# A two-block float32 layer on one core: the first output projection's banks, weight buffers and row order rearranged

## The reference

```python
x = _layer_norm(x, ln_emb_g, ln_emb_b)
proj = x @ w_in                                   # q_a k_a v_a f_a | q_r f_r i_r g_r
o_a = _rms_norm_heads(_fox_attention(q, k, v, logf_a))       # 8 heads of 64
o_r = _rms_norm_heads(_hgrn2_chunked(...)) * silu(g_r)       # 4 heads of 128
mix = concatenate([o_a, o_r]) @ w_o                          # 1024 x 1024
x = _layer_norm(ALPHA * x + mix, ln_mix_g, ln_mix_b)         # ALPHA = 2 ** 0.25
h = causal_depthwise_conv(x @ w_up)                          # 1024 x 5632, width 3
a, u = split(h)
x = _layer_norm(ALPHA * x + (gelu(a) * u) @ w_down, ln_ffn_g, ln_ffn_b)
x = second_block(x, ...)
```

## Time and profile before

| | us |
|---|---|
| median of three runs | 1674.93 (1673.72 to 1675.19) |
| the profiled execution, its own time | 1673.51 |
| its span, first to last instruction | 1671.7 |
| PE busy (matmuls) | 1591.8 |
| DVE busy | 1012.8 |
| ACT busy | 698.3 |
| POOL busy | 417.9 |

### The profile page before, as it was taken

The page is one execution under the profiler, slowest core; times in us unless marked ns, Lnnn a source line. Parts: engine busy times, 40 slices in busy tenths (PEclk is TensorE's granted clock), DMA queues, the critical chain, the costliest instruction groups (busy, mean ns, idle before and its releaser), DMA issues. The chain is left out here.

```text
span 1671.7 us, 21242 instructions
## 1 busy us (share of the span) xinstructions
PE 1591.8 (95%) x8600; PEld 1335.6 (80%) x8600; DVE 1012.8 (61%) x1443; ACT 698.3 (42%) x1012; POOL 417.9 (25%) x350
## 2 busy tenths in 40 slices
PE   5999988989999999999999999999799999999997
PEld 5778876767878888788888778887688899999886
DVE  6665546557977577433776544336864688886334
ACT  5644345543533243322542334444443654544222
POOL 0024302330621111100053012223432455551002
PEclk8999999999999899999999999999999999999999
DMA  7242212352244345222346423323444022234221
GB/s 291 101 143 85 76 63 76 113 203 101 83 170 160 143 151 200 103 101 83 117 152 252 126 76 100 108 81 107 176 148 182 26 102 102 102 114 146 94 76 51
DMA packets 47068, 203.93 MB, mean 122 GB/s; under 512 B 14352, under 2 KB 14736, under 8 KB 28346
## 3 DMA queue, kind: packets, MB, share of 16 engines
q1 hardware_dynamic: 37346, 171.84, 28.8%
q0 software_dynamic: 9088, 30.38, 5.3%
q10 hardware_dynamic: 536, 0.35, 0.1%
HBM read 181.56 MB, written 21.00 MB: 121 GB/s over the span
## 5 line engine op out<-in xcount | busy, mean ns | idle before, releaser
L557 PE MATMUL ps<-xh,whi 128*128 128x512 f32 (+1 forms) x1120 | 401.0, 358 | 5.7 <-DVE wlo L1801 5.3
L559 PE MATMUL ps<-xh,wlo 128*128 128x512 f32 (+1 forms) x1120 | 395.0, 353 | 0.0
L558 PE MATMUL ps<-xl,whi 128*128 128x512 f32 (+1 forms) x1120 | 393.6, 351 | 0.0
L1801 DVE TENSOR_TENSOR wlo<-raw,whi 128x2048 fp32r<-128x2048 f32 x93 | 233.3, 2509 | 137.7 <-ACT whi L1189 137.6
L1189 ACT ACTIVATE whi<-raw 128x2048 fp32r<-128x2048 f32 (+1 forms) x191 | 237.9, 1250 | 151.3 <-PE ps L559 104.3
L557 PEld LDWEIGHTS ps<-xh,whi 128*128 128x128 f32 x1120 | 212.1, 189 | 46.2 <-issue 11.6
L559 PEld LDWEIGHTS ps<-xh,wlo 128*128 128x128 f32 x1120 | 211.5, 189 | 31.4
L558 PEld LDWEIGHTS ps<-xl,whi 128*128 128x128 f32 x1120 | 212.8, 190 | 28.9
L2211 DVE SCALAR_TENSOR_TENSOR xr<-ps,pc,xr 128x511 f32<-128x511 f32 x88 | 65.2, 747 | 45.9 <-ACT xr L1189 44.3
L2619 POOL TENSOR_TENSOR act<-xr 128x512 f32<-128x512 f32 x22 | 39.2, 1782 | 204.6 <-DVE xr L2211 203.8
L2517 DVE TENSOR_TENSOR wlo<-raw,whi 128x512 fp32r<-128x512 f32 x98 | 77.7, 824 | 0.5 <-ACT whi L1189 0.5
(11 more groups left out here) (449 smaller groups left out, 3585.8 us busy)
## 6 DMA issues: line engine op xcount, KB each, us to landing
raw<-in_w_in SPq DMA_DIRECT2D x35, 1024.0 KB, 5.1
raw<-in_ffn_w SPq DMA_DIRECT2D x33, 1024.0 KB, 4.8
raw<-in_ada SPq DMA_DIRECT2D x24, 1024.0 KB, 4.8
raw<-in_w_up SPq DMA_DIRECT2D x22, 1024.0 KB, 4.8
raw<-in_w_down SPq DMA_DIRECT2D x11, 1024.0 KB, 4.7
xd<-X POOLq DMA_DIRECT2D x8, 512.0 KB, 7.7
td<-vr POOLq DMA_DIRECT2D x16, 256.0 KB, 3.6
raw<-td SPq DMA_DIRECT2D x4, 1024.0 KB, 5.4
```

The lines of the kernel that those rows point to most:

```text
L557: pe.e.matmul(o, lh, rh, start=start, stop=False)
L558: pe.e.matmul(o, lh, rl, start=False, stop=False)
L559: return pe.e.matmul(o, ll, rh, start=False, stop=stop)
L1801: up(ve.e.tensor_tensor(lo, raw[conv_at[j] % 3][:, :], hi.bitcast(F32), ALU.subtract), "wlo")
```

## The change

Six things.

1. **Banks.** The projection's column half 0 takes its four banks, and mix tile 7 its one, from the pool "attention" (as all of the attention's tiles); column half 1 goes on with "all". The bank that a take hands out, and so the signal that PE waits for, changes for all of the projection and for the transposes behind it.
2. **Mix tile 7** is turned after the first two row tiles of quarter `J_WO` and not after all four. On ACT the rounding of mix tiles 5 and 6 and the copy of `J_WO + 1` come before the last two evictions of the spectrum.
3. **Mix tiles 0 to 3** have their turn in steps 11 to 14 instead of 9 to 12, on PE, DVE and ACT.
4. **Buffers.** `J_WO + 3` and `J_UP + 2` get the place over `qa` and `ka` that `J_UP` had, and `J_UP` uses a shared pair.
5. **Row order on DVE.** Gain and bias, first half, second half, statistics and scale go by row tiles, interleaved, and not each step over all four tiles. `WO_RES` numbers the signals of the new order.
6. **Down operands.** The first three of `ah` and `al` are made ahead of the last pair's evictions.

The diff, cut to what the prediction speaks of:

```diff
-J_AHEAD = (J_UP, J_K2, J_UP2)
+J_AHEAD = (J_WO + 3, J_UP + 2, J_K2, J_UP2)
...
-                    if 9 <= i <= 12:
-                        pe.wait_ge(sig["rec"], i - 8)
-                        mix_turn(i - 9, tiles_of(orr, i - 9))
+                    if 11 <= i <= 14:
+                        pe.wait_ge(sig["rec"], i - 10)
+                        mix_turn(i - 11, tiles_of(orr, i - 11))
...
             rows_by(J_WO, wo_tiles(0), lambda kg, t: pe.wait_ge(sig["sp_lo"], split_no("mix", 4 * kg + 3)),
-                    between=lambda: last_mixed(3))
+                    after=lambda n: None if n else last_mixed(3), pool="attention")
             rows_last(J_WO + 2, wo_tiles(1), after_wo)
...
-                    if j == J_UP:
-                        ac.wait_ge(sig["pe"], at["w", J_WO])
+                    if j in (J_WO + 3, J_UP + 2):
+                        ac.wait_ge(sig["pe"], at["w", J_WO + 3 if j > J_WO + 3 else J_WO])
...
             head_squares(7, oa, 3)
-            spectrum(14)
+            mix_high(5)
             head_roots(ms_f[:, 24:32], 64, 8)
-            mix_high(5)
-            spectrum(15)
             mix_high(6)
             high(J_WO + 1)
+            spectrum(14)
+            spectrum(15)
             mix_high(7)
...
+                    if (j2, part) == (10, 1):
+
+                        ac.wait_ge(sig["ch_lo"], 20)
+                        ac.wait_ge(sig["act"], 3)
+                        for k in range(3):
+                            act(dn1[k][0][:, :], act1[:, k, :], ACT.Copy, "sp_hi")
...
+            gained(0)
+            gained(1)
+            wo_first(0)
+            wo_first(1)
+            gained(2)
+            low_parts(J_UP)
+            wo_stats(0)
+            gained(3)
+            inverse(1, 0)
+            wo_first(2)
+            wo_stats(1)
+            wo_first(3)
+            inverse(1, 1)
+            wo_stats(2)
+            inverse(1, 2)
             channels(4)
             channels(5)
             wo_stats(3)
...
+                    if (j2, part) == (10, 1):
+                        for k in range(3):
+                            low_part(dn1[k][1][:, :], act1[:, k, :], dn1[k][0][:, :], "down0", k)
```

More of the change, by code:

```diff
@@ L150 @@
 LAST = (0, 0), (1, 0), (0, 1), (1, 1), (2, 0), (2, 1), (3, 0), (3, 1)
+WO_RES = {k: n + 1 for n, k in enumerate(((0, 0), (1, 0), (0, 1), (2, 0), (1, 1), (3, 0), (2, 1), (3, 1)))}
 def weight_plan(ins, td):
@@ L474, in build @@
         raw_sem = [sig["raw0"], sig["raw1"], sig["raw2"]]
-        ahead = {J_UP: (flat(qa_r), flat(ka_r)), J_K2: (flat(qn_r), flat(qt_r)),
+        ahead = {J_WO + 3: (flat(qa_r), flat(ka_r)), J_UP + 2: (flat(qa_r), flat(ka_r)), J_K2: (flat(qn_r), flat(qt_r)),
                  J_UP2: (flat(cl), flat(act2_r[:, 0:4, :]))}
@@ L593, in tile, with rows_by @@
                 done(o, key)
-            def rows_by(j0, tiles, ready, after=None, between=None):
-                bs = [take(key, name, value) for key, name, value, *_ in tiles]
+            def rows_by(j0, tiles, ready, after=None, between=None, pool=None):
+                bs = [take(key, name, value, pool) for key, name, value, *_ in tiles]
                 for kg in range(2):
@@ L792, in gather, with mix_turn @@
                 done(m, ("ao", i))
-            def mix_turn(n, x):
-                b = take(("mix", n), "mx_m", n + 1)
+            def mix_turn(n, x, pool=None):
+                b = take(("mix", n), "mx_m", n + 1, pool)
                 turn(("mix", n), b, x)
@@ L847, in last_mixed @@
                 pe.wait_ge(sig["hn_x"], 5 + k)
-                mix_turn(4 + k, tiles_of(oa, k))
+                mix_turn(4 + k, tiles_of(oa, k), "attention")
             for k in (1, 2):
@@ L863, in wo_tiles @@
             def wo_tiles(cg):
-                return [(("wo", t, cg), "res", 4 * cg + t + 1, mix_hi, mix_lo, t) for t in range(4)]
+                return [(("wo", t, cg), "res", WO_RES[t, cg], mix_hi, mix_lo, t) for t in range(4)]
             def mix_rows(t):
@@ L1480, in scalar_program, with pieces @@
                         channels(u)
-            def pieces(inst, src, dn, ready, first):
+            def pieces(inst, src, dn, ready, first, begun=0):
                 def one(k):
@@ L1495, in one @@
                     act(dn[k % 4][0][:, :], src[:, k, :], ACT.Copy, "sp_hi")
-                for k in range(4):
+                for k in range(begun, 4):
                     one(k)
@@ L1502, in pieces @@
                         one(k + 4)
-            pieces(0, act1, dn1, "act", lambda k: k + 1)
+            pieces(0, act1, dn1, "act", lambda k: k + 1, begun=3)
             def rows_1(t):
@@ L2134, in beside_fox @@
                     head_scale(orr, i - 6, 1, ms_r[:, 4 * (i - 6):4 * (i - 6) + 4], 1)
-                if 9 <= i <= 12:
-                    mix(i - 9)
+                if 11 <= i <= 14:
+                    mix(i - 11)
                 if i in (13, 20, 28):
@@ L2174, in residual, with gained @@
                 up(ve.e.scalar_tensor_tensor(out=x, in0=x, scalar=ALPHA, in1=b[:, :], op0=ALU.mult, op1=ALU.add), "res")
-            low_parts(J_WO + 2)
+            low_parts(J_WO + 3)
             ve.wait_ge(sig["rows"], 64)
-            for t in range(4):
+            def gained(t):
                 ve.wait_ge(sig[("x0", "x1d", "x2", "x3")[t]], 32)
@@ L2243, in pieces @@
                         one(k + 4)
-            pieces(0, act1, dn1)
+            pieces(0, act1, dn1, begun=3)
             def down_stats(t):
```

14 lines of the change are left out of this document (4 added, 10 removed).

## The result

| | before | after |
|---|---|---|
| median of the runs beside each other | 1674.5 (1673.7 to 1675.2, 4 runs) | 1658.0 (1653.3 to 1659.1, 4 runs) |
| ratio, 95% interval | | 0.9895 (0.9884 to 0.9907) |
| the profiled execution, its own time | 1673.51 | 1653.27 |
| its span | 1671.7 | 1651.4 |

The time, 1658.0, lies inside the range (1651 to 1663) and 2 us above the forecast of 1656; the gain is 16.5 us.

The account below looks back on a forecast made before the run. PE, busy 95% of the span, was taken as the bound, so time is won only at its stops or low clock. 4.1 + 9.5 + 4.7 = 18.3 off the median gives 1656.6, forecast as 1656, range 1651 to 1663.

Parts of the forecast that it names:

- A: Attention: turning mix tiles 0 to 3 two steps later gains 4.1 us, bounds 2.5 and 6.5.
- B: First projection up to the up product: its changes gain 9.5 us, bounds 7.5 and 10.4.
- C: Down product's start: three operands made earlier remove PE's stop and low clock, 4.7 us, bounds 3.1 and 4.9.
- low part to 289.7: Attention, step 11: DVE's low part, taken as 2.93 us, ends at 289.7; PE then waits 0.6 for a bank.
- DVE as the bound: Attention, steps 11 to 15: DVE's work comes together, waits equal those removed; gain there 0.5, time 1660; chance 13%.
- the four-step sums: Attention, steps 9 to 12 and 13 to 16: each four steps would take 13 or 14 us.
- The rule on the port: Projection, mix tile 7: the page's exclusive lock would make PE wait 1.4 us, 1657.5 instead of 1656; forecast kept 1656.
- I take 379.7: Projection: the last broadcast row lands at 379.7, within 378 to 381.7, a loss of 0.4 us.
- Late rows: Projection: broadcast rows land at 381.7, DVE's list 2.4 late, PE waits over 3 us; 1658.5; chance 15%.
- That `J_WO + 3` has a place of its own changes nothing here: First projection: this weight buffer's separate place gains nothing, since both copies wait for the same point.
- given back in the up product: Up product: DVE and POOL, not PE, are the bound; the projection's gain falls to about 2, 1664; chance 4%.
- denser matmuls: Whole kernel: the denser PE is granted less clock; 0.015 less gives 1679; chance 1%.

Follow-up runs that it names:

- hold_pool: The kernel after, with POOL's spectrum additions held back until DVE's low part in step 11 and, at the attention's end, until mix tile 4 is read: 1652.65, ratio 0.9873.
- buffers_undone: The kernel after with the weight buffers of before (`J_UP` over `qa` and `ka`, `J_WO + 3` and `J_UP + 2` in shared pairs): 1660.32, ratio 0.9915.
- mix_only: The kernel before with only mix tiles 0 to 3 turned in steps 11 to 14: 1672.6, ratio 0.9994.
- down_only: The kernel before with only the first three down operands made ahead of the last evictions: 1670.81, ratio 0.998.
- projection_only: The kernel after without the later mix tiles and the earlier down operands, leaving the first projection's banks, buffers and row order: 1662.41, ratio 0.9936.
- after_again: The kernel after, unchanged, run again as the measure for its group: 1657.27, ratio 0.9901.

## Why the prediction was right, point by point

**The total** was right, and it was so in part because errors cancelled. By term: A 4.1, measured 1.2 to 1.4. B 9.5, measured 8.0 in the trace up to the up product (the shift goes from +1.2 to -6.8), and 1.5 more behind it, since PE no longer stops for `xl` and keeps its clock. C 4.7, measured 4.8 at its place and 3.1 in the median. And 2.6 us in the traces, 3.6 in the median, that no term had, from the second block's attention. That the 2.7 us missing from A and this gain elsewhere nearly cancel is luck.

**Part A, the failed step.** It was "low part to 289.7", which took DVE's 2.93 from the earlier trace rows and set it in a new place. The 2.93 from 292.74 was the last 0.8 of an addition of POOL's, from 292.25 to 293.53, and 2.1 of its own. Two steps on, PE being earlier, POOL has its additions at hand just behind the products, and both fall on the same low part: 0.6 until they begin, 2.5 for both, 2.2 for itself. From there the reasoning held. The rival *DVE as the bound* came near in its outcome (waits of 2.50 and 0.45 where there were 3.21, 0.32 and 0.45, and 1.2 us of gain, not 0.5), but not in its cause, DVE's own work coming together: `hold_pool` takes no work from DVE, and the 2.50 goes. Of the signs named, the four-step sums were to be 13 or 14 us: they are 14.9 and 13.2. The trace of before had the rows that would have told it: that addition, and DVE's low part of a mix tile, 0.69 alone, that took 2.00 while POOL's products of the earlier trace rows ran to 286.7.

```profile
285.25 2.00 DVE L1806 TENSOR_TENSOR gcr<-mx,qrr 128x512 fp32r<-128x512 f32 x1 [0.70 <-ACT qrr L1189]
...
292.25 1.28 POOL L2619 TENSOR_TENSOR spo<-spe,spo 128x512 f32<-128x512 f32 x1
```

**The rule on the port** was weighed against a row, and the row was misread. In all of them DVE ends when POOL's instruction has ended and DVE's own time, less some 0.14, has passed: 285.25 + 2.00 is POOL's end at 286.71 and 0.54 (0.69 alone), 360.00 + 1.52 of the earlier trace rows is POOL's end at 360.98 and 0.54, 292.74 + 2.93 is 293.53 and 2.14 (2.29 alone), 287.53 + 5.25 is 290.62 and 2.16. The traces agree with the Trainium skill, page "SBUF — State Buffer", sections Terms and "Who interferes with whom": an exclusive lock for a whole instruction. The place where I applied it came out well for another reason. At 366 DVE was first, and it was POOL that waited: DVE's low part of `J_WO + 1` took 2.29, POOL's addition 2.43 and not 1.28. DVE then lost 0.9 at the next row instead: the split of mix tile 7 took 1.59 and not 0.69, beside POOL's second addition, and still ended at 370.45, ahead of PE's asking at 371.37.

```profile
366.22 2.43 POOL L2641 TENSOR_TENSOR sps<-spe,spo 128x512 f32<-128x512 f32 x1 [13.12 <-ACT spo L1191]
...
368.86 1.59 DVE L1812 TENSOR_TENSOR grr<-mx,vrr 128x512 fp32r<-128x512 f32 x1 [0.70 <-ACT vrr L1191]
```

**Part B.** Up to column half 1 the working was exact: 10.45 sooner predicted, 10.4 measured (from +1.2 to -9.2), no stop, clock 1.00. The step that was off is "I take 379.7" for the landing of the last broadcast row. It landed at 383, 1.3 beyond the far bound of 381.7, as its issue was 1.8 later than worked out (the shift, and POOL's 2.43 and 1.29) and it took 10.2. That is the rival *Late rows*, with its 5.03 us on DVE and PE's wait of 2.53 at row tile 1 with low clock. "That `J_WO + 3` has a place of its own changes nothing here" was wrong: it is worth 3.8 us at this place by the trace of `buffers_undone`, since in a shared pair it waits for the end of column half 0 with all of DVE's row work behind it.

**Part C** was right at its place: no stop, and the fourth `ah` and the second weight piece in time. Whether its median of 3.1 is less than the 4.7 the runs can't tell.

**Not foreseen:** the turn of the banks in the second block; I followed the banks to the up product and no further. And the end of the attention, where the same wait for `pt` was 0.61 before and 2.25 after. The rows of DVE, ACT and POOL around it last as long in both traces (DVE's two scalings 2.36, POOL's additions 1.3 and 1.7). Before, PE's clock had fallen ahead of the wait, and the slower matmuls filled it; after, it fell behind it. By the shift this cost 1.6 us of the gain, in `mix_only` as in the kernel after, more than part A had brought. In `down_only` and `projection_only` PE stood the same 2.25 us, but its clock stayed at 1.00 on both sides and the shift didn't change. So it is not a price of part A alone; where the clock falls here differs from trace to trace. The row of before:

```profile
348.40:352.70 4.30, 3.70 (x19) 3.44 (x18) 3.50 (x7) 2.33 (x7) 3.32 (x3) 0.60 0.00 0
```

**The rivals not met:** nothing was given back in the up product (shift -6.8 at its start, -11.0 at its end, the difference being low clock that before has there and this trace of after has not; in `after_again` it ends at -8.7), and denser matmuls weren't granted less clock: 1.00 over 42 us.

## What to carry to other kernels

When an instruction is moved, its duration does not move with it: look up what the engine that shares its port does at the new time, and read a row of DVE or POOL that is longer than its kind as perhaps the other's instruction plus its own. A change in the number of takes from a pool shifts every later assignment; look at the first waits of each later stage, and try the turn by itself, since one line was worth 3.6 us here. What was gained by moving work can be gained again by moving the work that it now collides with: holding back POOL's additions at two places, issuing four transfers earlier and one gain sooner brought 7.9 us, half as much as the whole change.

## What the runs showed of the hardware

- DVE and POOL wait for each other by whole instructions, in both directions: 2.29 became 5.25 beside two additions, and 1.28 became 2.43 beside a low part. Which of two waiting ones comes first is not clear. At 288 to 290.6 both of POOL's additions went ahead of a DVE instruction that the record has begin at 287.53, when POOL was issuing a transfer and no addition ran yet; at 285.25 the third of POOL's products ended 0.2 us later and the fourth still went first. But in before DVE went between the two at 360.00 to 361.52, and POOL's second took 1.71, not 1.28. No run here tells these cases apart.

```profile
360.94 1.71 POOL L2619 TENSOR_TENSOR spo<-spo,spe 128x512 f32<-128x512 f32 x1
```

- PE's clock falls without a stop too. In all traces there is one place where PE is busy all the time with 64 matmuls of one column, and the clock falls within it and stays low 3 to 5 us behind it: in before 0.72 over 10.00 us with PE busy for 10.00, and 0.52 over the next 4.80.

```profile
562.50:572.50 10.00, 10.00 (x66) 9.99 (x65) 6.26 (x7) 2.58 (x2) 2.26 (x2) 0.72 0.49 188
572.50:577.30 4.80, 4.80 (x13) 3.69 (x13) 0.23 (x2) 0.00 (x0) 0.00 (x0) 0.52 0.60 234
```

- Whether the clock falls behind a given stop of 2.2 to 2.3 us differs between executions of one program (at 848 in one trace of the kernel after and not in the other), at 1.5 to 1.6 us each. The kernel before spread over 2 us in its runs, the kernel after over 6.
